# Sliding-window scores of the two later query blocks from stacked high and low parts, and the token rows reloaded later

## The chip, the cores and the metric

One core of one Trainium2 chip runs the whole program. The number is the device time of one execution in microseconds (us); the median of several executions is compared. The engines are TensorE (PE, its weight loads are listed apart as PEld), VectorE (DVE), ScalarE (ACT), GpSimd (POOL) and SyncE (SP, which here only issues DMAs).

## The reference, cut to what matters

512 tokens of width 1024 go through one decoder block. After an RMSNorm and an input projection come two groups of 8 query heads on 2 key heads each, head width 64. One is banded attention with a window of 128 and a sink per head; the other has a compressed, a selected and a window-512 branch. The part that is changed is the score product of the first group:

```
s = einsum('bnqhgd,bnkhd->bnhgqk', qb, kb) * (dh ** -0.5)     # 128 queries x 256 keys
s = where(mask, s, -inf)
p = softmax(concatenate([s, sink]))[..., :-1]
```

Then `x = x + mixed @ w_out`, and `x = x + peer_ffn(rmsnorm(x))`: products with 2 x 128 x 128 expert rows and a top-16 retrieval. All of it is float32.

## The kernel before

**Precision.** A product of two float32 tiles is either one plain float32 matmul, or some matmuls of type fp32r. For the latter an operand is split into a high part (ScalarE copies it to an fp32r tile) and a low part (the rest, by a subtraction). A head has only 64 rows, so the rows of a 128-row operand can hold a query's high part on one half and its low part on the other ("stacked"). Against the key's high part on both halves, and then the key's low part on both halves, two matmuls give the whole product.

**The attention loop.** 96 units run in one software pipeline, `UNITS`: query block qb = 0 to 3, then the branches SWA (the local attention), SEL, WIN, then 8 heads. Unit s = 24 qb + 8 branch + head. The score width is 128 or 256 for SWA (at most two key blocks), and 128 (qb + 1) for the others. So SWA units are s = 0 to 7, 24 to 31, 48 to 55 and 72 to 79. At step s:

- TensorE issues the scores of unit s into `bank[s % 3]` (`query_keys`: L1598 if packed, two matmuls; L1600 if plain, one matmul that the trace shows as two passes; then the mask, L1602), after `exp_done` of unit s-3. Then it transposes the probabilities of unit s-3 (L1671) and multiplies those of unit s-5 with the values (L1687). Between these lie the compressed branch's steps (L1632, L1697, L1703) and transposes of finished rows (L1646).
- VectorE takes the maximum of unit s (L1142 for SWA and then a minimum with the sink, L1143; L1146 for the others), and at even s copies the transposed probabilities of unit s-3 out of PSUM (L1211). Every eighth step it closes a group of 8 units (`finish`, L1114 to L1133). The compressed branch has L1177 and L1183.
- ScalarE takes the exponential of unit s (L761), and at odd s copies the transposed probabilities of unit s-3 (L780).

**Packing before.** Only SEL and WIN of query blocks 2 and 3 (widths 384 and 512) are packed: q in `qp`, k in `k_hi` and `k_lo`. The parts are made inside the loop, `PARTS` of them (4 of q, then 8 of k) at the steps `PACK_AT` = 12, 14, ..., 34. At each, ScalarE writes the high part on 64 partitions x 512 at the head of its step, before exp(s) (L741, L745), and GpSimd, in the order of `PARTS`, subtracts it to give the low part (L528, L533). For k, GpSimd waits until all four high parts of a key head are there (`pack_hi >= i + 4 - n`), so its subtractions come in runs of four. The first packed unit, s = 56, waits for all of `pack_lo`.

**Token rows.** `xt`, 16 KB of each partition, holds the token rows at the start. While attention runs it is first scratch of the compressed branch (`cx`, `hid_raw`, `hrep`). SyncE reloads x into it (`load_x`, L369, 2 MB) once `hrep` has been used (`cmp_ps >= 2`, step 6), then waits for the last score (`s_done >= 96`) and loads the next weight tile (L409). The first reader of the reloaded rows is the residual addition after the output projection, L1249.

Of the kernel before, what the change touches and what calls it, by code (L numbers as in the profile page):

```python
# [99 lines left out]
C_AT = [50 + 6 * qb for qb in range(TB)]  # L100
C_LATE = 2
PACKED = 2 * P
PARTS = [(w, g, n) for w in ("q", "k") for g in range(GROUPS) for n in (range(2) if w == "q" else range(4))]
PACK_AT = {12 + 2 * i: i for i in range(len(PARTS))}
M_AT = {74 + 5 * b + 2 * half: (b, half) for b in range(TB - 1) for half in range(2)}
W4_AT = {57 + 2 * k: k for k in range(KC)}

# [29 lines left out]
def build(nc, x, x_t, pos, params, consts, consts_b, consts_h, wts, wgate, w1, w2, subkeys, norms, down, rows, up, y):  # L137
# [80 lines left out]
    cx_parts = [place(f"cx_parts{i}", [P, LP, 2, GROUPS, NC], F32R, xt_at + i * 8192) for i in range(2)]  # L218
    w1_lo = [place("w1k_lo", [P, LP, CMP_HIDDEN], F32R, after_w), place("w1v_lo", [P, LP, CMP_HIDDEN], F32R, w1v_at)]
    w1_hi = [place("w1k_hi", [P, LP, CMP_HIDDEN], F32R, base + 32768), place("w1v_hi", [P, LP, CMP_HIDDEN], F32R, base)]  # L220
    glog_T = place("glog_T", [2 * N_GATES, T], F32, scratch)
    hid_raw = [place(f"hid_raw{i}", [2 * GROUPS * NC, 2 * CMP_HIDDEN], F32, xt_at + (1 + i) * 2048) for i in range(2)]
    hrep = place("hrep", [P, GROUPS * 2, 4, CP], F32, xt_at)
# [130 lines left out]
    with nc.Block() as block:  # L354

        @block.sync
        def _(sp):
# [32 lines left out]
            for i in range(1, TILES_IN + TILES_OUT + 2):  # L390
                if i == TILES_IN + TILES_OUT:
                    sp.wait_ge(S("mixed_done"), TB)
                    for e in range(DR):
                        load_down(e)
                    sp.dma_start(h_row[:], norms[1:2].partition_broadcast(P).rearrange("p o d -> p (o d)"))\
                      .then_inc(S("late_loaded"), 16)
                    sp.dma_start(sk[:], subkeys.rearrange("p (s k) -> p s k", s=2)).then_inc(S("late_loaded"), 16)
                if i >= 2:
                    used, count = tile_used(i - 2)
                    sp.wait_ge(S(used), count)  # L400
                if i == TILES_IN + 1:
                    sp.wait_ge(S("hrep_done"), 1)
                    sp.wait_ge(S("cmp_ps"), 2)
                    load_x()
                    sp.wait_ge(S("s_done"), len(UNITS))
                if i == TILES_IN:
                    sp.wait_ge(S("hid_done"), 2)
                w_i = wts[i].rearrange("p (k c) -> p k c", k=KC)
                sp.dma_start(w_raw[i % 2][:], w_i).then_inc(S(f"w_loaded{i % 2}"), 16)  # L409
                if i == 1:  # L410
                    sp.dma_start(wg_raw[:], wgate.rearrange("p (k c) -> p k c", k=KC)).then_inc(S("wg_loaded"), 16)
# [78 lines left out]
        def _(pool):  # L490
# [32 lines left out]
            for i, (what, g, n) in enumerate(PARTS):  # L523
                own = slice(DH * g, DH * g + DH)
                if what == "q":
                    other = slice(DH * (1 - g), DH * (1 - g) + DH)
                    pool.wait_ge(S("pack_hi"), i + 1)
                    nc.gpsimd.tensor_tensor(qp[g][other, 2 * n:2 * n + 2], qT[own, 1, 2 * n:2 * n + 2, PACKED:T],  # L528
                                            f32(qp[g][own, 2 * n:2 * n + 2]), ALU.subtract).then_inc(S("pack_lo"), 1)
                else:  # L530
                    to, br = slice(DH * (n // 2), DH * (n // 2) + DH), n % 2
                    pool.wait_ge(S("pack_hi"), i + 4 - n)
                    nc.gpsimd.tensor_tensor(k_lo[g][to, br], kT[own, 2 + br], f32(k_hi[g][own, br]), ALU.subtract)\  # L533
                        .then_inc(S("pack_lo"), 1)
# [54 lines left out]
        def _(act):  # L589
# [137 lines left out]
            for s in range(len(UNITS) + 13):  # L727
# [9 lines left out]
                if s in PACK_AT:  # L737
                    what, g, n = PARTS[PACK_AT[s]]
                    own = slice(DH * g, DH * g + DH)
                    if what == "q":  # L740
                        nc.scalar.activation(qp[g][own, 2 * n:2 * n + 2], qT[own, 1, 2 * n:2 * n + 2, PACKED:T], ACT.Copy)\  # L741
                          .then_inc(S("pack_hi"), 1)
                    else:
                        to, br = slice(DH * (n // 2), DH * (n // 2) + DH), n % 2
                        nc.scalar.activation(k_hi[g][to, br], kT[own, 2 + br], ACT.Copy).then_inc(S("pack_hi"), 1)  # L745
# [730 lines left out]
        def _(pe):  # L1476
# [102 lines left out]
            def query_keys(s):  # L1579
# [3 lines left out]
                n = width(qb, br)  # L1583
                k0 = (qb + 1) * P - n
                tok = slice(qb * P, (qb + 1) * P)
                if n > PACKED:
                    if s == min(u for u in range(len(UNITS)) if width(*UNITS[u][:2]) > PACKED):
                        pe.wait_ge(S("pack_lo"), len(PARTS))
                elif br == SWA:
                    q = (q_g1 if g else qT)[:, 0, j, tok]  # L1590
                else:
                    q = q_g1[:, 1, j, tok] if g else q_g0[:, j, tok]
                if s >= 3:
                    pe.wait_ge(S("exp_done"), s - 2)
                if n > PACKED:
                    q = qp[g][:, j, qb * P - PACKED:(qb + 1) * P - PACKED]
                    for x, kk in enumerate((k_hi[g], k_lo[g])):
                        nc.tensor.matmul(bank[s % 3][:, 0:n], q, kk[:, K_OF[br] - 2, k0:k0 + n], start=(x == 0), stop=False)  # L1598
                else:
                    nc.tensor.matmul(bank[s % 3][:, 0:n], q, kT[:, K_OF[br], k0:k0 + n], start=True, stop=False)  # L1600
                mw = n if br == SWA else P
# [338 lines left out]
```

## Time and profile before

| | |
|---|---|
| median of 3 runs | 1538.78 us (1537.42 to 1542.04) |
| the profiled execution, its own time | 1537.43 us |
| its span in the trace | 1535.6 us |
| TensorE / VectorE / ScalarE / GpSimd busy | 98% / 80% / 41% / 35% |
| attention loop in the trace | about 118 to 252 us |
| TensorE's granted clock | 1.00 in every stretch of the loop, the mean 0.997 |

The profiled execution lies 1.35 us below the median, and 1.8 us of it lie outside the span. Busy shares are averages over very unlike stages. "PE busy" in a window includes modelled ends of matmuls, so distances between the starts of matmuls are the safer measure of TensorE's pace.

### The profile page before, as it was taken

The numbers are of one execution on the slowest core, as the hardware profiler recorded it, in microseconds if no ns is written. First come the engines' busy times: TensorE is split into PE (matmuls) and PEld (weight loads), VectorE is DVE, ScalarE is ACT, GpSimd is POOL, SyncE is SP. The second block draws the span as 40 slices with busy tenths as digits, with TensorE's granted clock in tenths as the row PEclk, the third lists the DMA queues.
The fourth block names the chain that finished last, engine by engine and source line by source line (L and its number), as shares of the span: only waits on it lengthen the run. The fifth ranks groups of instructions, "written<-read, shape, count | busy, mean of one in ns | idle before, by whom it ended". The sixth has DMA issues, their size and how long they took to land.

```text
span 1535.6 us, 22620 instructions
## 1 busy us (share of the span) xinstructions
PE 1510.3 (98%) x8483; PEld 1347.4 (88%) x8483; DVE 1229.3 (80%) x2264; ACT 626.5 (41%) x1048; POOL 538.1 (35%) x359
## 2 busy tenths in 40 slices
PE   9999999999999999999999999999999999999997
PEld 6887888798889999998888888999999999999996
DVE  5567885439999999984776777888888889888885
ACT  6247565333222346663333333333333333333334
POOL 0322101055756720002111112555555555555521
PEclk9999999999999999999999999999999999999999
DMA  7302003224323548989999989999999999999961
GB/s 309 145 26 86 1 2 127 95 91 131 122 66 104 178 156 315 341 313 357 307 302 307 308 289 344 367 363 369 361 359 368 364 372 363 359 375 353 372 237 65
DMA packets 148508, 378.85 MB, mean 247 GB/s; under 512 B 11792, under 2 KB 76688, under 8 KB 145456
## 3 DMA queue, kind: packets, MB, share of 16 engines
q1 hardware_dynamic: 100544, 202.01, 37.8%
q0 software_dynamic: 37200, 138.56, 24.6%
q10 hardware_dynamic: 10656, 36.85, 6.5%
q8 instruction: 68, 1.11, 0.3%
q14 instruction: 40, 0.33, 0.1%
HBM read 338.50 MB, written 38.86 MB: 246 GB/s over the span
## 4 chain that ended last, share of the span: by engine, by line
PE 71%; DVE 24%; ACT 2%; DMA 2%; issue 1%; SPq 0%; DVEq 0%; ACTq 0%
PE bank L1847 22%; PE bank L1755 15%; PE bank L1853 11%; PE bank L1480 8%; PE bank L1762 7%; PE bank L1687 2%; DVE oh L1379 2%; DVE gp L1387 2%; DVE gp L1384 2%; DVE oh L1382 2%; DVE cand L1317 1%; PE bank L1671 1%; DVE d_lo L1368 1%; DVE key L1272 1%; DVE ti L1291 1%
## 5 line engine op out<-in xcount | busy, mean ns | idle before, releaser
L1755 PE MATMUL bank<-h_hi,d_hi 128*128 128x384 f32 x1024 | 349.8, 342 | 1.1 <-DVE h_lo L1233 1.1
L1755 PE MATMUL bank<-h_lo,d_hi 128*128 128x384 f32 x1024 | 345.3, 337 | 0.0
L577 POOL DMA_INDIRECT p_in<-rows,p_row x128 | 161.7, 1263 | 402.3 <-DVE p_dot L1406 183.3
L577 POOL DMA_INDIRECT p_in<-up,p_row x128 | 172.2, 1345 | 191.3 <-DVE p_dot L1406 97.0
L1762 PE MATMUL bank<-h_hi,d_lo 128*128 128x384 f32 x1024 | 200.1, 338 | 0.0
L1755 PEld LDWEIGHTS bank<-h_hi,d_hi 128*128 128x128 f32 x1024 | 192.9, 188 | 4.0 <-issue 1.3
L1755 PEld LDWEIGHTS bank<-h_lo,d_hi 128*128 128x128 f32 x1024 | 192.8, 188 | 3.2
L1847 PE MATMUL bank<-u_hi,w_hi_e 128*128 128x512 f32 x750 | 192.2, 391 | 0.3 <-DVE w_lo_e L1431 0.3
L1847 PE MATMUL bank<-u_hi,w_lo_e 128*128 128x512 f32 x750 | 191.0, 390 | 0.0
L1853 PE MATMUL bank<-u_lo,w_hi_e 128*128 128x512 f32 x750 | 190.9, 390 | 0.0
L1762 PEld LDWEIGHTS bank<-h_hi,d_lo 128*128 128x128 f32 x1024 | 180.9, 188 | 0.0
L1412 DVE SCALAR_TENSOR_TENSOR xt<-p_in,p_w,xt 128x1024 f32<-128x1024 f32 x128 | 164.0, 1281 | 5.6
L1847 PEld LDWEIGHTS bank<-u_hi,w_lo_e 128*128 128x128 f32 x750 | 140.8, 188 | 30.7
L1853 PEld LDWEIGHTS bank<-u_lo,w_hi_e 128*128 128x128 f32 x750 | 140.8, 188 | 29.2
L895 ACT ACTIVATE a_e<-bank 128x384 f32<-128x384 f32 x69 | 34.0, 492 | 323.6 <-PE bank L1762 323.6
L1363 DVE TENSOR_TENSOR u_lo<-u_raw,u_hi 128x1024 fp32r<-128x1024 f32 x128 | 156.4, 1223 | 11.0 <-ACT u_hi L869 10.6
L1426 DVE TENSOR_TENSOR a_e<-a_e,g_e 128x384 f32<-128x384 f32 x128 | 71.3, 557 | 115.6 <-ACT a_e L895 63.8
L1847 PEld LDWEIGHTS bank<-u_hi,w_hi_e 128*128 128x128 f32 x750 | 139.7, 188 | 25.8 <-ACT u_hi L869 0.7
L1406 DVE CUSTOM_DVE_ANT_0 p_in<-p_in,h_row 128x1024 f32<-128x1024 f32 x128 | 153.2, 1219 | 0.0
L538 POOL TENSOR_TENSOR d_lo<-d_raw,d_hi 128x1024 fp32r<-128x1024 f32 x35 | 89.2, 2556 | 171.4 <-ACT d_hi L793 171.4
L900 ACT ACTIVATE w_hi_e<-a_e 128x384 fp32r<-128x384 f32 x128 | 67.4, 526 | 194.9 <-DVE a_e L1426 191.6
L793 ACT ACTIVATE d_hi<-d_raw 128x1024 fp32r<-128x1024 f32 x128 | 134.4, 1052 | 29.9 <-ACT f_act L823 24.1
(289 smaller groups left out, 2462.5 us busy)
## 6 DMA issues: line engine op xcount, KB each, us to landing
d_raw<-down SPq DMA_DIRECT2D x128, 512.0 KB, 6.3
u_raw<-up SPq DMA_DIRECT2D x128, 512.0 KB
gates_dram<-ev ACTq DMA_DIRECT2D x12, 2048.0 KB, 7.5
g_e<-gates_dram SPq DMA_DIRECT2D x32, 768.0 KB
w_raw<-wts SPq DMA_DIRECT2D x9, 2048.0 KB, 8.6
act_dram<-f_act ACTq DMA_DIRECT2D x59, 192.0 KB
a_e<-act_dram SPq DMA_DIRECT2D x59, 192.0 KB
xt<-x_in SPq DMA_DIRECT2D x2, 2048.0 KB, 11.7
```

Source lines behind the costliest of these rows:

```text
L538: nc.gpsimd.tensor_tensor(d_lo[f % DR][:], d_raw[f % DR][:], f32(d_hi[f % DH_R][:]), ALU.subtract)\
L577: pool.indirect_dma_start(out=p_in[n % GR][:], out_offset=None, in_=rows if kind == "D" else up.rearrange("n p d -> (n p) d"), in_offset=b ...
L793: nc.scalar.activation(d_hi[e % DH_R][:], d_raw[e % DR][:], ACT.Copy).then_inc(S("d_hi_done"), 1)
L1363: V.tensor_tensor(u_lo[e % DR][:], u_raw[e % DR][:], f32(u_hi[e % UH][:]), ALU.subtract)\
L1406: V.tensor_tensor_reduce(out=rows_in[:], in0=rows_in[:], in1=h_row[:], scale=1.0, scalar=0.0, op0=ALU.mult, op1=ALU.add, accum_out=p_dot[: ...
L1412: V.scalar_tensor_tensor(xt[:, TDB], rows_in[:], p_w[:, p:p + 1], xt[:, TDB], ALU.mult, ALU.add)\
L1426: V.tensor_tensor(a_v, a_v, g_e[n % 3][:, :, e % GB], ALU.mult).then_inc(S("w_mul"), 1)
L1480: m = nc.tensor.matmul(out, a, b, start=(n == 0 and j == 0), stop=(n == last and j == 2))
L1755: nc.tensor.matmul(bank[6 + e % 2][:, 0:TD], d_hi[e % DH_R][:, k], h[:, k, 0:TD], start=(k == j == 0), stop=False)
L1762: m = nc.tensor.matmul(bank[6 + e % 2][:, 0:TD], d_lo[e % DR][:, k], h_hi[:, k, 0:TD], start=False, stop=(k == KC - 1))
L1847: nc.tensor.matmul(bank[2 * b + half][:], w[e % 3][:, b * P:(b + 1) * P], u_hi[e % UH][:, half * COLS:(half + 1) * COLS], start=(e == 0 an ...
L1853: m = nc.tensor.matmul(bank[2 * b + half][:], w_hi_e[e % 3][:, b * P:(b + 1) * P], u_lo[e % DR][:, half * COLS:(half + 1) * COLS], start=F ...
```

## The change

It packs the SWA scores of query blocks 2 and 3 too (units 48 to 55 and 72 to 79). Their parts, 4 of q (`qs`) and 4 of k (`ks_hi`, `ks_lo`), go ahead of the 12 old ones, so that `PACK_AT` now has the 20 steps 10, 12, ..., 48: new ones at 10 to 24, the old q parts at 26 to 32, the old k parts at 34 to 48. Unit 48 waits for 8 low parts, and unit 56 for all 20. The new tiles take the room of `xt`, so ScalarE waits for `cmp_ps >= 2` before the first, and SyncE reloads x only after the last SWA score (`s_done >= 80`).

```diff
--- before.py
+++ after.py
@@ -100,8 +100,9 @@
 C_AT = [50 + 6 * qb for qb in range(TB)]
 C_LATE = 2
 PACKED = 2 * P
-PARTS = [(w, g, n) for w in ("q", "k") for g in range(GROUPS) for n in (range(2) if w == "q" else range(4))]
-PACK_AT = {12 + 2 * i: i for i in range(len(PARTS))}
+PARTS = [(w, g, n) for w in ("qs", "ks") for g in range(GROUPS) for n in range(2)]
+PARTS += [(w, g, n) for w in ("q", "k") for g in range(GROUPS) for n in (range(2) if w == "q" else range(4))]
+PACK_AT = {10 + 2 * i: i for i in range(len(PARTS))}
 M_AT = {74 + 5 * b + 2 * half: (b, half) for b in range(TB - 1) for half in range(2)}
 W4_AT = {57 + 2 * k: k for k in range(KC)}
 
@@ -218,6 +219,9 @@
     cx_parts = [place(f"cx_parts{i}", [P, LP, 2, GROUPS, NC], F32R, xt_at + i * 8192) for i in range(2)]
     w1_lo = [place("w1k_lo", [P, LP, CMP_HIDDEN], F32R, after_w), place("w1v_lo", [P, LP, CMP_HIDDEN], F32R, w1v_at)]
     w1_hi = [place("w1k_hi", [P, LP, CMP_HIDDEN], F32R, base + 32768), place("w1v_hi", [P, LP, CMP_HIDDEN], F32R, base)]
+    qs = [place(f"qs{g}", [P, HPG, T - PACKED], F32R, xt_at + g * 4096) for g in range(GROUPS)]
+    ks_hi = [place(f"ks_hi{g}", [P, T], F32R, xt_at + 8192 + g * 2048) for g in range(GROUPS)]
+    ks_lo = [place(f"ks_lo{g}", [P, T], F32R, xt_at + 12288 + g * 2048) for g in range(GROUPS)]
     glog_T = place("glog_T", [2 * N_GATES, T], F32, scratch)
     hid_raw = [place(f"hid_raw{i}", [2 * GROUPS * NC, 2 * CMP_HIDDEN], F32, xt_at + (1 + i) * 2048) for i in range(2)]
     hrep = place("hrep", [P, GROUPS * 2, 4, CP], F32, xt_at)
@@ -401,6 +405,7 @@
                 if i == TILES_IN + 1:
                     sp.wait_ge(S("hrep_done"), 1)
                     sp.wait_ge(S("cmp_ps"), 2)
+                    sp.wait_ge(S("s_done"), STEP_QB * (TB - 1) + HEADS)
                     load_x()
                     sp.wait_ge(S("s_done"), len(UNITS))
                 if i == TILES_IN:
@@ -527,6 +532,17 @@
                     pool.wait_ge(S("pack_hi"), i + 1)
                     nc.gpsimd.tensor_tensor(qp[g][other, 2 * n:2 * n + 2], qT[own, 1, 2 * n:2 * n + 2, PACKED:T],
                                             f32(qp[g][own, 2 * n:2 * n + 2]), ALU.subtract).then_inc(S("pack_lo"), 1)
+                elif what == "qs":
+                    other = slice(DH * (1 - g), DH * (1 - g) + DH)
+                    pool.wait_ge(S("pack_hi"), i + 1)
+                    nc.gpsimd.tensor_tensor(qs[g][other, 2 * n:2 * n + 2],
+                                            (q_g1 if g else qT)[own, 0, 2 * n:2 * n + 2, PACKED:T],
+                                            f32(qs[g][own, 2 * n:2 * n + 2]), ALU.subtract).then_inc(S("pack_lo"), 1)
+                elif what == "ks":
+                    to = slice(DH * n, DH * n + DH)
+                    pool.wait_ge(S("pack_hi"), i + 2 - n)
+                    nc.gpsimd.tensor_tensor(ks_lo[g][to], kT[own, 0], f32(ks_hi[g][own]), ALU.subtract)\
+                        .then_inc(S("pack_lo"), 1)
                 else:
                     to, br = slice(DH * (n // 2), DH * (n // 2) + DH), n % 2
                     pool.wait_ge(S("pack_hi"), i + 4 - n)
@@ -737,7 +753,16 @@
                 if s in PACK_AT:
                     what, g, n = PARTS[PACK_AT[s]]
                     own = slice(DH * g, DH * g + DH)
-                    if what == "q":
+                    if PACK_AT[s] == 0:
+                        act.wait_ge(S("cmp_ps"), 2)
+                    if what == "qs":
+                        nc.scalar.activation(qs[g][own, 2 * n:2 * n + 2],
+                                             (q_g1 if g else qT)[own, 0, 2 * n:2 * n + 2, PACKED:T], ACT.Copy)\
+                          .then_inc(S("pack_hi"), 1)
+                    elif what == "ks":
+                        to = slice(DH * n, DH * n + DH)
+                        nc.scalar.activation(ks_hi[g][to], kT[own, 0], ACT.Copy).then_inc(S("pack_hi"), 1)
+                    elif what == "q":
                         nc.scalar.activation(qp[g][own, 2 * n:2 * n + 2], qT[own, 1, 2 * n:2 * n + 2, PACKED:T], ACT.Copy)\
                           .then_inc(S("pack_hi"), 1)
                     else:
@@ -1583,19 +1608,26 @@
                 n = width(qb, br)
                 k0 = (qb + 1) * P - n
                 tok = slice(qb * P, (qb + 1) * P)
-                if n > PACKED:
+                packed = n > PACKED or (br == SWA and qb * P >= PACKED)
+                if packed:
                     if s == min(u for u in range(len(UNITS)) if width(*UNITS[u][:2]) > PACKED):
                         pe.wait_ge(S("pack_lo"), len(PARTS))
+                    if s == STEP_QB * PACKED // P:
+                        pe.wait_ge(S("pack_lo"), 4 * GROUPS)
                 elif br == SWA:
                     q = (q_g1 if g else qT)[:, 0, j, tok]
                 else:
                     q = q_g1[:, 1, j, tok] if g else q_g0[:, j, tok]
                 if s >= 3:
                     pe.wait_ge(S("exp_done"), s - 2)
-                if n > PACKED:
-                    q = qp[g][:, j, qb * P - PACKED:(qb + 1) * P - PACKED]
-                    for x, kk in enumerate((k_hi[g], k_lo[g])):
-                        nc.tensor.matmul(bank[s % 3][:, 0:n], q, kk[:, K_OF[br] - 2, k0:k0 + n], start=(x == 0), stop=False)
+                if packed:
+                    late = slice(qb * P - PACKED, (qb + 1) * P - PACKED)
+                    if br == SWA:
+                        q, parts = qs[g][:, j, late], [kk[:, k0:k0 + n] for kk in (ks_hi[g], ks_lo[g])]
+                    else:
+                        q, parts = qp[g][:, j, late], [kk[:, K_OF[br] - 2, k0:k0 + n] for kk in (k_hi[g], k_lo[g])]
+                    for x, kk in enumerate(parts):
+                        nc.tensor.matmul(bank[s % 3][:, 0:n], q, kk, start=(x == 0), stop=False)
                 else:
                     nc.tensor.matmul(bank[s % 3][:, 0:n], q, kT[:, K_OF[br], k0:k0 + n], start=True, stop=False)
                 mw = n if br == SWA else P
```

## Rows read from the trace of the kernel before

**Rows 1.** The page: engines and lines of the chain that ended last.
```profile
PE 71%; DVE 24%; ACT 2%; DMA 2%; issue 1%; SPq 0%; DVEq 0%; ACTq 0%
```

**Rows 2.** Windows: stretch, length, busy us of PE, PEld, DVE, ACT, POOL; clock, DMA.
```profile
161.00:177.00 16.00, 16.00 (x122) 14.09 (x121) 13.25 (x41) 10.34 (x38) 0.00 (x0) 1.00 0.01 2
177.00:183.00 6.00, 4.61 (x37) 3.96 (x35) 5.32 (x14) 1.73 (x6) 0.00 (x0) 1.00 0.00 1
...
207.00:217.00 10.00, 10.00 (x83) 9.14 (x81) 6.89 (x19) 6.06 (x18) 0.00 (x0) 1.00 0.00 1
```

**Rows 3.** Timeline of PE, a plain SWA unit: start, us, line, operation.
```profile
207.71 0.65 PE L1600 MATMUL bank<-kT,qT 128*128 128x256 f32 x2
208.19 0.27 PE L1602 MATMUL bank<-cstb 128*128 128x256 bf16 x1
```

**Rows 4.** Timeline of PE, fp32r matmuls of 256 and of 384 columns.
```profile
107.10 0.38 PE L1513 MATMUL bank<-w1v_hi,cx_parts 128*124 128x256 f32 x1
107.32 0.28 PE L1513 MATMUL bank<-w1v_lo,cx_parts 128*124 128x256 f32 x1
107.44 0.28 PE L1513 MATMUL bank<-w1v_hi,cx_parts 128*124 128x256 f32 x1
...
188.79 0.42 PE L1598 MATMUL bank<-k_hi,qp 128*128 128x384 f32 x1
189.05 0.33 PE L1598 MATMUL bank<-k_lo,qp 128*128 128x384 f32 x1
189.22 0.23 PE L1602 MATMUL bank<-cstb 128*128 128x128 bf16 x1
```

**Rows 5.** The chain in order of time, around units 53 and 77: start, us, what.
```profile
177.26 0.12 PE bank L1602
...
182.26 0.41 PE bank L1671 x2
...
216.77 0.44 DVE nmax L1142
```

**Rows 6.** Timeline of DVE and POOL, and line L533's durations (ns, min/median/max).
```profile
143.55 0.67 DVE L1143 TENSOR_TENSOR nmax<-nmax,nsink 128x1 f32<-128x1 f32 x1
144.59 0.97 DVE L1143 TENSOR_TENSOR nmax<-nmax,nsink 128x1 f32<-128x1 f32 x1
...
157.40 1.23 DVE L1114 TENSOR_TENSOR coef<-rsum,es 128x8 f32<-128x8 f32 x1
...
141.72 5.05 POOL L533 TENSOR_TENSOR k_lo<-kT,k_hi 64x512 fp32r<-64x512 f32 x4 [5.51 <-ACT k_hi L745]
154.50 5.34 POOL L533 TENSOR_TENSOR k_lo<-kT,k_hi 64x512 fp32r<-64x512 f32 x4 [7.73 <-ACT k_hi L745]
...
L533 POOL TENSOR_TENSOR k_lo<-kT,k_hi x8: 1257/1266/1530, 141.7 to 158.6; 64x512 fp32r<-64x512 f32 x8
```

**Rows 7.** Timeline of PE, the masks of units 29, 30 and 40 to 42.
```profile
144.75 0.27 PE L1602 MATMUL bank<-cstb 128*128 128x256 bf16 x1
...
146.36 0.27 PE L1602 MATMUL bank<-cstb 128*128 128x256 bf16 x1
...
159.94 0.22 PE L1602 MATMUL bank<-cstb 128*128 128x128 bf16 x1
...
161.85 0.22 PE L1602 MATMUL bank<-cstb 128*128 128x128 bf16 x1
...
163.06 0.22 PE L1602 MATMUL bank<-cstb 128*128 128x128 bf16 x1
```

**Rows 8.** Line L745's durations, and a row of ACT's timeline (idle before it).
```profile
L745 ACT ACTIVATE k_hi<-kT x8: 620/628/632, 136.0 to 153.8; 64x512 fp32r<-64x512 f32 x8
...
131.86 0.37 ACT L761 ACTIVATE pr<-bank,nmax 128x128 f32<-128x128 f32 x1 [0.42 <-DVE nmax L1146]
```

**Rows 9.** DMA issue of x (KB each, us to landing), and its first reader.
```profile
xt<-x_in SPq DMA_DIRECT2D x2, 2048.0 KB, 11.7
...
L1249 DVE TENSOR_TENSOR xt<-xt,bank x8: 674/686/689, 266.0 to 302.3; 128x512 f32<-128x512 f32 x8
```

## The prediction

> **What bounds the kernel now.** I first read the chain of waits of the page: TensorE holds 71% of it and VectorE 24% [rows 1]. The attention loop is a small part of the span, but nothing after it can start without it, so a microsecond gained or lost there should be one at the end. The question is which engine sets the pace of each stretch of the loop. For that I read busy time by stretch, the chain piece by piece, and the starts of the mask matmuls, one for each unit.
>
> The reader is to see three things. Between 161 and 177 us TensorE is never idle, while VectorE is busy 13.25 of 16 us; between 177 and 183 us this turns round, 4.61 of 6 us for TensorE and 5.32 for VectorE [rows 2]. The chain changes engine there: from 177.4 us, the scores of unit 53 being ready, to 182.26 us it runs over VectorE (maximum, closing of a group, compressed branch), and TensorE then continues with the transposes of step 56. The same happens behind unit 77, at 216.77 us [rows 5]. So of the 16 units to be changed, 48 to 53 and 72 to 77 are on the chain with their TensorE time, 12 in all, and 54, 55, 78 and 79 are not.
>
> The third thing is small rows that are far too long. L1143, a minimum of one column, took 0.67 and 0.97 us, and L1114, eight columns, took 1.23 us [rows 6]. Normal is about 0.16 us for either (the 0.67 and 0.97 are above it by 0.51 and 0.81, the 1.23 by 1.07, in sum 2.4 us). All three lie inside a run of GpSimd subtractions, 141.72 to 146.77 and 154.50 to 159.84 us, and each ends where one of the subtractions ends (1.27 us each). They read both operands from SBUF; VectorE's instructions with one operand in PSUM, beside them, keep their length. I take it that such a VectorE instruction waits out the GpSimd instruction that is running. It also goes the other way: one L533 took 1530 ns where 1266 is the median [rows 6].
>
> The Trainium skill, page "SBUF — State Buffer", section "Who interferes with whom", says the same: a VectorE instruction with two SBUF inputs contends with a GpSimd instruction that reads SBUF, and the second to issue waits for the first to end. The trace agrees (0.67, 0.97 and 1.23 us, and 1530 ns). By that rule, which names no other case, the change would be charged as in the forecast below; were it not to hold, as in the first rival.
>
> **What a packed unit costs TensorE.** A plain unit takes 208.19 - 207.71 = 0.48 us from its first pass to its mask [rows 3]. For two fp32r matmuls of 256 columns there are two neighbours. In the compression, coming from plain matmuls, the first takes 0.22 us to the start of the second, and that 0.12 us: 0.34. The packed pair of 384 columns takes 0.26 + 0.17 = 0.43 us [rows 4]. The pair has 256 columns, so I take 0.34 us, and for the slightly earlier start behind L1687 nothing: a gain of 0.14 us a unit. The bound on the bad side is the 384-column price, a gain of 0.05 us; on the good side two matmuls at the later spacing, 0.24 us, a gain of 0.24. On the chain, 12 units: 12 x 0.14 = **1.7 us gained** (0.6 to 2.9). The mask is unchanged. In block 3 the cover for this is good: VectorE is busy only 6.89 of 10 us between 207 and 217 [rows 2], so six units' 0.8 us should be kept. In block 2 VectorE has 16 - 13.25 us free before it takes over, and the other six units' 0.8 us is kept only if nothing is added to VectorE.
>
> **ScalarE.** Eight packs of 0.63 us are added [rows 8]; since the list starts at 10 and ends at 48, the steps that had none before are 10 and 36 to 48. Queued behind a pack is exp(s), and the transposes and scores of step s+3 wait for that. The pack at 10 delays ScalarE by about 0.4 us in a stretch where it has little room, but the idle 0.42 us before exp at 131.86 us takes it up [rows 8]: 0.1 us, at most 0.6. At 36 to 48 ScalarE is busy 10.34 of 16 us [rows 2]; a pack every second step adds 0.63 per 2.3 us, 4.3 us over that stretch, which makes 14.7 of 16. It fits, barely, because exp(s) is wanted only three steps later. I put 0 on it, at most 1.
>
> **GpSimd's removed runs.** In the kernel before, subtractions run in the two groups of rows 6. What TensorE lost by them can be read off the masks: unit 30 came 1.61 us after unit 29 where 1.21 is the pace, and unit 41 came 1.91 us after 40 where 42 follows 41 by 1.21 [rows 7]. That is 0.40 + 0.70 = 1.1 us of the 2.4 us that VectorE lost, a share of 0.46. With the old k parts moved on, the second run no longer meets L1114 of step 37, and the first is replaced by single subtractions. If all is removed, **1.1 us gained**.
>
> **GpSimd's new places.** There are now 20 subtractions, 25.3 us at 1.27. They come singly after the packs at 10 to 16 and at 26 to 32, in pairs after 20 and 24, and in runs of four (about 5.1 us) after 40 and 48. VectorE's instructions with two SBUF operands at those steps, counted in the code: step 13 L1114; step 21 L1118; steps 24 to 31 eight L1143; steps 29 and 32, L1118, L1131, L1214 (15 or so in stretches where GpSimd works about half the time: 12 in number, 6 hit); steps 41 to 44 four L1183 and step 45 L1118; steps 48 to 52 five L1143 and L1192 (11, inside or at the edge of the runs: 10 hit). Sixteen hits at the mean wait of three before, 2.4/3 = 0.8 us, would be 12.8 us; the mean of a wait that begins anywhere in 1.27 us is 0.63, which gives 10 us. I take 0.63, as a wait is at most one subtraction. With the share 0.46 that reached TensorE before, **4.6 us lost**. The bounds: nothing, if VectorE's slack takes all up (its lag behind the masks was absorbed in more than half of the cases); 10 us if all reach TensorE. Most of it I expect at steps 41 to 52. There the pace was TensorE's, and a run that blocks L1183 and then L1143 turns it into VectorE's: one subtraction and one blocked 0.4 us instruction make 1.67 us for a step that took 1.2. ScalarE's packs lie in the same steps.
>
> **The waits on the parts.** Unit 48 needs the eighth low part, made about 20 steps earlier. Unit 56 needs the twentieth. Unit 48 lies some 6 to 7 us ahead of the mask of 53 at 177.26, so the last pack ends near 172 and four subtractions near 177; the scores of unit 56 come less than 2 us ahead of its step's transposes at 182.26 [rows 5]. The wait costs nothing, with about 3 us to spare; if the last run were stretched by more than that, TensorE would stand behind it with all transposes of the step queued.
>
> **The reload.** It is issued after unit 79, about 4 us behind the row at 216.77 [rows 5], lands 11.7 us later, near 233, and is first read at 266.0 us [rows 9]. SyncE has nothing queued between but the wait for the last score, after which its weight load is issued as before. 0 us, with some 30 us of cover.
>
> **The sum.** -1.7 (TensorE) + 0.1 (ScalarE) - 1.1 (old runs) + 4.6 (new runs) = +1.9 us. The profiled execution's 1537.43 would become 1539.3; on the median of 1538.78 it is 1540.7. I give **1540.5 us**. 0.3% of this kernel is 4.6 us; this is about what a measurement can tell from no change.
>
> **The rivals.**
> - *The gain lands* (chance 0.28). VectorE's slack and three units of distance absorb the waits on GpSimd, as they absorbed 54% of them before. For it: GpSimd's new singles are short and VectorE is idle up to 3 us of 10 in block 3. Against: VectorE had 2.75 us free in 16 where the runs now fall. The time: 1538.78 - 1.7 - 1.1 = 1536.0, with the good bound of a pair 1534.8.
> - *Slower by more than 0.3%* (0.07). One mechanism: the waits of VectorE on GpSimd reach TensorE nearly in full at steps 41 to 56, since ScalarE's packs have used up the slack there. 16 hits of 0.63 give 10 - 2.7 = +7.3 us, 1546.1. It decides from 11 or 12 hits on that pass through in full (4.6 + 2.7 = 7.3 us). Against it: less than half passed before.
> - *The pair is no cheaper* (0.07). At 0.43 us or more for a pair the change brings TensorE 0.6 us or less, and the lock stays: 1538.78 - 0.6 - 1.1 + 4.6 + 0.1 = 1541.8.
>
> **How the numbers follow.** The forecast has the remaining 0.58. The range reaches from near the first rival's time to between the forecast and the second: 1536.0 to 1544.0. All but the second rival lie within 4.6 us of now; a measurement's own scatter adds a little at either edge. Faster by over 0.3%: 0.03; within 0.3%: 0.90; slower by over 0.3%: 0.07.
>
> **What would show it.** In the profile after: L1598 with 256-column pairs about 0.34 us from first to mask; L1183 and L1143 rows above their 0.4 and 0.16 us wherever a GpSimd row lies beside them, some ten or more; L1114 of step 37 back at 0.16 us; TensorE's masks of units 41 to 52 further apart than 1.2 us; block 3's SWA units 0.14 us quicker each; the loop's end a little later than 252 us, or earlier if the first rival holds. The prediction is wrong if VectorE's long rows are few, if they are many and TensorE's masks keep their pace, or if anything behind the loop changes its length.

## The result and the profile after

| | before | after |
|---|---|---|
| median | 1538.74 us (1537.39 to 1542.04, 10 runs) | 1544.3 us (1541.51 to 1547.15, 10 runs) |
| the profiled execution, its own time | 1537.43 us | 1544.3 us |
| its span | 1535.6 us | 1542.5 us |
| attention loop, first mask to last | 129.2 us | 133.2 us |
| busy share TensorE / VectorE / ScalarE / GpSimd | 98 / 80 / 41 / 35% | 98 / 80 / 41 / 35% |

The ratio is 1.0034, 95% interval 1.0024 to 1.0043. The kernel became slower, clear of the scatter. Whether by more or by less than 0.3%, the size that the prediction set as its limit, the interval doesn't tell. The forecast of 1540.5 us lies 3.8 us below the median, and the range ended at 1544.0, 0.3 us below it.

The page's chain of the changed kernel, by engine, is nearly the same (before: [rows 1]):

```profile
PE 70%; DVE 24%; DMA 2%; issue 2%; ACT 1%; SPq 0%; ACTq 0%; DVEq 0%
```

The windows answer better to the question (columns as in [rows 2]):

```profile
124.00:131.00 7.00, 7.00 (x51) 6.60 (x52) 3.90 (x16) 4.13 (x20) 1.02 (x1) 0.76 0.01 2
...
161.00:177.00 16.00, 15.18 (x116) 12.78 (x115) 15.55 (x38) 12.51 (x38) 7.21 (x6) 1.00 0.01 2
177.00:183.00 6.00, 3.84 (x28) 3.35 (x28) 4.31 (x10) 2.49 (x10) 3.20 (x3) 1.00 0.01 1
...
207.00:217.00 10.00, 10.00 (x87) 9.29 (x86) 9.12 (x22) 6.61 (x21) 0.00 (x0) 1.00 0.01 2
...
306.00:314.00 8.00, 6.35 (x30) 5.92 (x29) 4.78 (x10) 2.32 (x5) 0.00 (x0) 0.79 0.73 265
```

Between 161 and 177 us VectorE went from 13.25 to 15.55 of 16 us busy, and TensorE, never idle before [rows 2], now is. Two stretches, at 124 and at 306 us, have a granted clock of 0.76 and 0.79.

The timeline of TensorE, around the steps 50 to 56 and in block 3:

```profile
175.22 0.36 PE L1630 MATMUL bank<-ks_hi,qs 128*128 128x256 f32 x1
...
175.42 0.28 PE L1630 MATMUL bank<-ks_lo,qs 128*128 128x256 f32 x1
...
175.54 0.28 PE L1634 MATMUL bank<-cstb 128*128 128x256 bf16 x1
...
177.50 0.41 PE L1703 MATMUL bank<-cst,pr 128*128 128x128 f32 x2 [0.47 <-ACT pt L805]
...
179.54 0.41 PE L1703 MATMUL bank<-cst,pr 128*128 128x128 f32 x2 [0.82 <-DVE pt L1236]
...
181.21 1.13 PE L1735 MATMUL bank<-vbd,c_pT 128*128 128x256 f32 x4 [0.87 <-ACT c_pT L796]
...
187.60 0.41 PE L1703 MATMUL bank<-cst,pr 128*128 128x128 f32 x2 [1.75 <-DVE pt L1236]
```

A packed unit takes 0.20 us to its second matmul and 0.12 to its mask, 0.32 in all, where a plain one takes 0.48 [rows 3]. In brackets stands TensorE's idle time: 0.47, 0.82 and 0.87 us at steps 51 to 53. From mask to mask, compared with before, the step of unit 53 is longer by 1.91 us, 25 by 0.63, 33 by 0.56, 49 by 0.50, 52 by 0.49 and 47 by 0.44; 41 is shorter by 0.76 us, 30 by 0.31, and 72 to 79 by 0.18 each, of which unit 81 gives back 0.36.

What VectorE does at these steps, and GpSimd beside it:

```profile
164.51 1.28 DVE L1208 TENSOR_TENSOR c_sc<-c_sc,cst 128x248 f32<-128x248 f32 x1
...
174.40 0.16 DVE L1168 TENSOR_TENSOR nmax<-nmax,nsink 128x1 f32<-128x1 f32 x1
...
175.70 0.78 DVE L1168 TENSOR_TENSOR nmax<-nmax,nsink 128x1 f32<-128x1 f32 x1
...
177.00 0.77 DVE L1217 TENSOR_TENSOR c_coef<-c_sum,gates 128x32 f32<-128x32 f32 x1
...
178.25 0.81 DVE L1168 TENSOR_TENSOR nmax<-nmax,nsink 128x1 f32<-128x1 f32 x1
...
164.25 5.48 POOL L549 TENSOR_TENSOR k_lo<-kT,k_hi 64x512 fp32r<-64x512 f32 x4 [7.73 <-ACT k_hi L770]
175.19 5.08 POOL L549 TENSOR_TENSOR k_lo<-kT,k_hi 64x512 fp32r<-64x512 f32 x4 [5.46 <-ACT k_hi L770]
```

L1168 is the minimum with the sink (L1143 before). At 174.40 us, before the run of subtractions, it takes 0.16 us; inside the run it takes 0.78 and 0.81. In all 14 VectorE rows of the loop are too long, by 9.40 us in sum, where before there were three and 2.4 us [rows 6]. The chain in order of time runs over these rows until TensorE's product L1735 of step 53. Of the L1168 row at 178.25 it has 0.07 us, and the rest of that row stands in it as "issue", time for which the profile shows no wait:

```profile
175.70 0.78 DVE nmax L1168
...
177.00 0.78 DVE c_coef L1217
177.80 0.43 DVE nmax L1167
178.25 0.07 DVE nmax L1168
...
180.89 0.28 ACT c_pT L796
181.21 1.13 PE bank L1735 x4
```

The reload stays covered, by these three rows of after (SyncE's timeline, the list of DMA issues, whose last column is the time to landing, and the first reader L1274): issued at 223.13 us, it is there 11.2 us later, 36 us before 270.4.

```profile
223.13 0.38 SPq L373 DMA_DIRECT2D xt<-x_in  x1
...
xt<-x_in SPq DMA_DIRECT2D x2, 2048.0 KB, 11.2
...
L1274 DVE TENSOR_TENSOR xt<-xt,bank x8: 675/686/689, 270.4 to 306.7; 128x512 f32<-128x512 f32 x8
```

### The profile page after: what moved, and what is told of

Read it like the earlier page. It is cut to its first block, busy times and chain, and to the rows that moved or that the text cites. A ratio compares the mean times of both kernels' runs of the same rounds, so it can differ in the third digit from the quotient of the medians.

```text
span 1542.5 us, 22638 instructions
## 1 busy us (share of the span) xinstructions
PE 1512.1 (98%) x8483; PEld 1349.2 (87%) x8483; DVE 1235.2 (80%) x2264; ACT 630.4 (41%) x1056; POOL 547.6 (35%) x367
## 3 DMA queue, kind: packets, MB, share of 16 engines
q8 instruction: 68, 1.11, 0.3%
## 4 chain that ended last, share of the span: by engine, by line
PE 70%; DVE 24%; DMA 2%; issue 2%; ACT 1%; SPq 0%; ACTq 0%; DVEq 0%
PE bank L1879 22%; PE bank L1787 15%; PE bank L1885 11%; PE bank L1505 8%; PE bank L1794 7%; PE bank L1719 2%; DVE oh L1404 2%; DVE gp L1412 2%; DVE oh L1407 2%; DVE gp L1409 2%; DVE cand L1342 1%; DVE d_lo L1393 1%; DMA w_raw<-wts 1%; PE bank L1703 1%; DVE key L1297 1%
## 6 DMA issues: line engine op xcount, KB each, us to landing
xt<-x_in SPq DMA_DIRECT2D x2, 2048.0 KB, 11.2
```

## The experiments

The table has all runs; "loop" is first mask to last in the one trace, in us, "at full clock" the same without the excess of the steps that lay in a stretch of lower granted clock (against the same steps of before, or for after_again of after), and "long rows" counts VectorE's over-long rows in the loop with their excess in us. The ratio is to the kernel before on the same chip, with its interval. Two cautions: the kernel before against itself came to 0.9992 (before_again), so a ratio within 0.001 of 1 says little; and the choice of the steps that count as slowed by the clock moves a value at full clock by up to 0.7 us (for after_again it would be 131.2 if unit 57, which came sooner behind the stretch, were left out).

| run | ratio | loop | at full clock | long rows |
|---|---|---|---|---|
| before | 1 | 129.2 | 129.2 | 3, 2.4 |
| after | 1.0034 [1.0024, 1.0043] | 133.2 | 131.8 | 14, 9.4 |
| after_again | 1.0030 [1.0017, 1.0043] | 132.8 | 131.9 | 14, 9.4 |
| before_again | 0.9992 [0.9982, 1.0002] | 130.5 | 129.2 | 3, 2.4 |
| reload_late | 0.9991 [0.9982, 1.0000] | 130.6 | 129.3 | 3, 2.4 |
| low_memset | 0.9993 [0.9984, 1.0002] | 128.5 | 127.1 | 0 |
| sink_scalar | 1.0025 [1.0016, 1.0034] | 135.2 | 130.2 | 6, 4.5 |
| plain_48 | 1.0024 [1.0016, 1.0033] | 134.9 | 132.0 | 14, 9.3 |
| singles | 1.0017 [1.0005, 1.0030] | 133.1 | 130.1 | 11, 5.7 |
| singles_scalar | 1.0021 [1.0012, 1.0030] | 129.6 | 129.6 | 6, 2.7 |
| block3_scalar | 1.0017 [1.0006, 1.0027] | 133.9 | 128.8 | 3, 2.2 |
| block3_moved | 1.0008 [0.9999, 1.0017] | 132.8 | 130.0 | 4, 2.4 |
| before_fix | 1.0009 [1.0000, 1.0018] | 128.9 | 128.9 | 2, 0.7 |
| delay_only | 1.0034 [1.0024, 1.0044] | 137.6 | not worked out | 3, 2.4 |

The theory: nearly all of the loss is VectorE's operations with two operands in SBUF waiting behind GpSimd's subtractions. The rivals: the reload, the packed pair itself, ScalarE's packs, and the granted clock.

**The reload alone (reload_late).** The kernel before with one line added:

```diff
                     sp.wait_ge(S("cmp_ps"), 2)
+                    sp.wait_ge(S("s_done"), STEP_QB * (TB - 1) + HEADS)
                     load_x()
```

> The kernel before with the later reload of x alone. The yardstick is the distance from the mask of unit 0 to that of unit 95 in the trace: 129.23 us before; 133.22 us with the change, of which 1.4 us lie in units 7 to 9 at a granted clock of 0.72 (131.8 us without these). Theory (waits of VectorE on GpSimd): the reload is hidden, loop 129.2 us, time within 1 us of before, ratio 0.9993 to 1.0007. Rival (the reload or its absence from 125 us costs something): the stretch at 124 to 130 us runs at the lower clock again, +1.4 us, or the residual additions behind the loop start late, ratio above 1.001.

The ratio is 0.9991, as good as the 0.9992 of the unchanged kernel. The stretch of lower clock near 124 us, the rival's sign, stood in this trace, but it stands in before_again too, without the line. The reload costs nothing that shows.

**The low parts without reading (low_memset).** The whole change, but GpSimd's subtractions of all four kinds become memsets; so the low parts of all packed scores are left out of the result. One of the four edits:

```diff
-                    nc.gpsimd.tensor_tensor(k_lo[g][to, br], kT[own, 2 + br], f32(k_hi[g][own, br]), ALU.subtract)\
+                    nc.gpsimd.memset(k_lo[g][to, br], 0.0)\
                         .then_inc(S("pack_lo"), 1)
```

> The change with all 20 low parts left out: GpSimd fills them with zeros (it writes, and reads nothing) in the same order and with the same waits. ScalarE's 20 packs and TensorE's pairs stay. Theory (VectorE's instructions with two SBUF operands wait for GpSimd's reads): no long VectorE rows, L1168 at 0.16 us and L1208 at 0.40 us throughout; the loop falls from 131.8 to 125.5 to 127 us (before's 1.2 us of stalls and up to 2.6 us of TensorE's gain come out), ratio to before 0.997 to 0.9985. Rival (ScalarE's eight more packs set the pace): the loop stays at 131 us or more, ratio 1.001 to 1.003.

The timeline of VectorE and GpSimd, this run:

```profile
173.78 0.20 DVE L1214 TENSOR_TENSOR c_coef<-c_sum,gates 128x32 f32<-128x32 f32 x1
...
174.47 0.16 DVE L1165 TENSOR_TENSOR nmax<-nmax,nsink 128x1 f32<-128x1 f32 x1
...
172.34 2.03 POOL L546 MEMSET k_lo<- 64x512 f32 x4 [7.50 <-ACT k_hi L767]
```

Beside a run of memsets (172.34 to 174.37) the same product with the gates takes 0.20 us instead of 0.77, and no row of the loop is long. The list of TensorE's waits in the loop, first of after, then of this run:

```profile
PE bank L1703 <- DVE pt L1236: 4.8, 8, 1.7
...
PE bank L1703 <- ACT pt L805: 2.1, 3, 1.2
...
PE bank L1735 <- ACT c_pT L796: 1.1, 2, 0.9
```

```profile
PE bank L1700 <- DVE pt L1233: 2.4, 3, 1.7
PE bank L1700 <- ACT pt L802: 1.6, 2, 1.2
...
PE bank L1732 <- ACT c_pT L793: 0.8, 2, 0.5
```

With the waits gone the loop at full clock is 4.7 us shorter than after's, 2.1 us shorter than before's, and the ratio is 0.9993 instead of 1.0034: 0.41% or 6.3 us. The loop came near its 125.5 to 127; the ratio missed its 0.997 to 0.9985. The memsets are shorter too (0.51 us each against 1.27), but TensorE waited for no low part in either kernel. The pair, the eight packs and the later parts are all still in it, so none of them is the loss. Two things differ beside the waits and no run separates them: the shorter GpSimd instructions, and zeros in the place of the low parts, which TensorE multiplies. For the loop, the runs below with true low parts point the same way.

**The sink's minimum with a scalar operand (sink_scalar).**

```diff
-                        V.tensor_tensor(nmax[:, s:s + 1], nmax[:, s:s + 1], nsink[:, h:h + 1], ALU.min)\
+                        V.tensor_scalar(nmax[:, s:s + 1], nmax[:, s:s + 1], nsink[:, h:h + 1], None, ALU.min)\
```

> The change, with the minimum of SWA's maximum and the sink (L1168) written so that the sink is a scalar operand, not a second tensor from SBUF. Theory: L1168 is at its normal length beside GpSimd's rows, L1208, L1217 and L1143 still wait; units 48 to 53 lose less, loop 131.8 to between 129.5 and 130.8 us. Rival (ScalarE's packs): 131.8 us as it is.

VectorE's timeline and GpSimd's:

```profile
178.09 0.83 DVE L1217 TENSOR_TENSOR c_coef<-c_sum,gates 128x32 f32<-128x32 f32 x1
...
179.41 0.21 DVE L1168 TENSOR_SCALAR nmax<-nmax,nsink 128x1 f32<-128x1 f32 x1
...
176.35 5.07 POOL L549 TENSOR_TENSOR k_lo<-kT,k_hi 64x512 fp32r<-64x512 f32 x4 [5.47 <-ACT k_hi L770]
```

Inside one and the same run of subtractions, the operation with two tensors waits (0.83 us) and the one with a tensor and a scalar does not (0.21 us; all 32 lie between 0.212 and 0.215). The loop at full clock is 1.6 us shorter than after's. The Trainium skill, page "SBUF — State Buffer", section "Who interferes with whom", draws the line at the same place, two SBUF inputs against a GpSimd instruction that reads SBUF and not against one that only writes it; both runs agree (0.21 us here, 0.16 us beside the memset). But the ratio is 1.0025, its interval overlaps that of after: see the clock, below.

**Query block 2 plain (plain_48).**

```diff
-                packed = n > PACKED or (br == SWA and qb * P >= PACKED)
+                packed = n > PACKED or (br == SWA and qb == TB - 1)
```

> The change with units 48 to 55 as plain products again, all parts still made; block 3 packed. Theory: between units 48 and 56 VectorE sets the pace, so TensorE's gain there was worth nothing, and the loop stays within 0.4 us of 131.8. Rival (TensorE's gain of 0.18 us a unit landed in block 2 as well): six to eight units, 1.1 to 1.4 us more, 132.9 to 133.2 us.

All parts are still made. The loop at full clock is 132.0 us against 131.8: packing block 2's eight units is worth 0.2 us, since VectorE sets the pace there, while block 3's eight steps are 1.46 us shorter in after (0.18 each), or 1.1 with what unit 81 gives back. Unit 81 does so in every run that packs block 3, plain_48 among them, and in none that doesn't.

**Subtractions one at a time (singles, singles_scalar).** The key parts are ordered so that each subtraction needs only its own high part; the second has the scalar minimum as well.

```diff
-                    pool.wait_ge(S("pack_hi"), i + 4 - n)
+                    pool.wait_ge(S("pack_hi"), i + 1)
```

> The change, with GpSimd's subtractions each right behind its own pack instead of in pairs and runs of four (the order of the packs within a key head is turned for that). The same 20 subtractions, 20 packs and pairs. Theory (what counts is which VectorE instructions with two SBUF operands GpSimd's subtractions fall on): L1208 and L1168 of units 49 to 52 are hit less than now, L1202 of steps 37 to 40 more; sum of the waits 5 to 8 us against 9.4, loop 131.8 to 129.5 to 131.3 us without stretches of lower clock. Rival (ScalarE's packs): 131.8 as it is.

> The same, and the sink as a scalar operand as in sink_scalar. Theory: only L1202, L1208, L1217 and the closings of groups can still wait; loop 128 to 130 us, near before's 129.2. Rival (ScalarE): 131 or more.

Runs of four broken up take the sum of the waits from 9.4 to 5.7 us and the loop at full clock from 131.8 to 130.1; with the scalar minimum 2.7 and 129.6. The ratios, 1.0017 and 1.0021, stay above 1.

**Only block 3 (block3_scalar, block3_moved).** Block 2's scores plain, six new parts instead of eight, behind the old ones, and the scalar minimum; the second moves them to steps at which VectorE was expected to have fewer operations with two tensors, and has the second key head's subtractions single.

```diff
-PACK_AT = {10 + 2 * i: i for i in range(len(PARTS))}
+PACK_AT = {12 + 2 * i if i < OLD else (46, 48, 50, 60, 62, 64)[i - OLD]: i for i in range(len(PARTS))}
```

(block3_scalar has `46 + 2 * (i - OLD)` there.)

> A candidate to beat both: only units 72 to 79 are packed. The 12 old parts stay at steps 12 to 34, and six new ones (2 of q for the last 128 tokens, 4 of k) go to steps 46 to 56; the sink is a scalar operand. Theory: TensorE's 8 x 0.18 us of block 3 stay (1.4 us less 0.4 given back at unit 81), the waits of L1143 in units 27 to 29 go, the one on the closing at step 37 stays, new subtractions may hit the c_coef product, the closing at step 53 and its additions (0 to 1.5 us): loop 127 to 129 us against 129.2, ratio 0.998 to 1.0. Rival (ScalarE's packs): loop 129.2 or more.

> Only block 3's scores are packed (query block 2 keeps its plain products); the six low parts that block 3 needs are made at other steps (46, 48, 50, 60, 62 and 64), the sink's minimum goes to VectorE as an operation with one tensor and a scalar, and key head 1's subtractions stay single. My theory (the price of the change is the wait of VectorE's two-tensor operations behind GpSimd's subtractions, and it counts where the maxima stand behind it): few or no long VectorE rows, the loop at the full granted clock 127 to 127.5 us against 129.2, and 0.9985 of the time before if no stretch of lower clock is added. The rival (TensorE's short idle stretches cost through the granted clock, wherever work moves): the loop at full clock is shorter but the ratio stays at 1.000 or above.

block3_scalar comes to 128.8 us at full clock, within its 127 to 129, but its ratio of 1.0017 missed the 0.998 to 1.0. block3_moved missed its 127 to 127.5: the last parts fell on the closing of a group at step 64. Its VectorE and GpSimd:

```profile
192.28 1.80 DVE L1229 TENSOR_TENSOR xs<-xs,o_tmp 128x512 f32<-128x512 f32 x1
...
194.47 1.28 DVE L1247 TENSOR_TENSOR w_lo<-w_raw,w_hi 128x512 fp32r<-128x512 f32 x1
...
192.26 2.94 POOL L545 TENSOR_TENSOR ks_lo<-kT,ks_hi 64x512 fp32r<-64x512 f32 x2 [17.12 <-ACT ks_hi L765]
```

Their excess is 1.11 and 0.60 us over the usual 0.69 and 0.68, and the steps of units 63 and 64 are longer by 1.10 and 0.60: here, with nothing between, all of it reached TensorE. Even so its ratio, 1.0008, is the lowest of all versions that pack anything with true low parts.

**The repair without the packing (before_fix).** The kernel before with the scalar minimum, and the second key head's subtractions single.

```diff
-                    pool.wait_ge(S("pack_hi"), i + 4 - n)
+                    pool.wait_ge(S("pack_hi"), i + 1 if g else i + 4 - n)
```

> The kernel before, with no packing of the two later blocks; only the sink's minimum written with one tensor and a scalar, and key head 1's subtractions single. My theory: the loop at full clock 127.9 to 128.2 us against 129.2, and a ratio near 0.999. The rival: as in the run with the whole change, the time is taken back by stretches of lower clock, and the ratio is 1.000 to 1.002.

Units 30 and 41 came 0.40 and 0.76 us sooner, 33 and 34 took 0.36 back, and the loop was 0.3 us shorter, not 1.0. Two VectorE rows are long there, at 146.80 and 147.96 us; in low_memset, which has no such rows, 33 and 34 take nothing back. The ratio is 1.0009, so the forecast of 0.999 missed. So no version found beats the kernel before.

**A small stall alone (delay_only).** The kernel before, with 18 additions on VectorE at step 58, on a tile that nothing reads any more.

> The kernel before, with 18 chained additions on a dead tile put into VectorE's step 58, some 4 us in which TensorE runs dry and nothing else is changed. The question is why the change costs 5.3 us by the medians where its loop is only 2.6 us longer at equal clock. Theory (a later second half meets a lower clock once more often, near 310 us): loop +3.3 to 4.3 us, the granted clock falls between 306 and 316 us in this trace as with the change, mean clock over its runs 0.0005 to 0.001 below before's, time up by 1 to 1.5 us more than the loop. Rival (the extra belongs to the change itself): time up by as much as the loop, clock as before.

Its windows:

```profile
190.00:195.00 5.00, 2.82 (x23) 2.37 (x22) 4.48 (x18) 0.65 (x3) 0.00 (x0) 1.00 0.00 0
195.00:202.00 7.00, 6.30 (x30) 5.37 (x30) 5.99 (x13) 4.37 (x12) 0.00 (x0) 0.53 0.01 2
```

TensorE was idle 2.2 of 5 us and then ran at a granted clock of 0.53, near the lower of its two levels. 30 matmul rows lie in those 7 us, where 153 to 170 lie in 22 us at full clock. The ratio is 1.0034: no subtraction was added here and no row became long, and yet it costs what the whole change costs, 5.2 us. TensorE's waits for the copied probabilities there are 3.6 us, against 1.4 in the kernel before. The theory missed in three of its terms: the loop of this trace is 8.4 us longer, not 3.3 to 4.3 (4.9 us at units 61 to 65 and 3.5 at units 3 to 10, around a stretch of half clock such as other traces have near 124 us); the clock near 310 us stayed at 1.00; and the mean clock is 0.0019 lower, not 0.0005 to 0.001. The rival, the clock as before, missed too.

**Both kernels once more (after_again, before_again).**

> The changed kernel once more, for the scatter of a profile. If the stretches of lower granted clock belong to the kernel, its trace has them again near 125 and 310 us, and the ratio is again 1.003 to 1.004. If they fall by chance, they stand elsewhere or are missing, with the loop at 131 to 133 us.

> The kernel before once more. If the stretches of lower clock belong to the change, none near 125 and 310 us here, the loop 129.2 us and the ratio 1.000. If they fall by chance, one stands near 125 us here too, as in two other kernels with the block's work unchanged, and the ratio is still within 0.001 of 1.

The same windows, first before_again, then after_again:

```profile
124.00:131.00 7.00, 7.00 (x52) 6.68 (x52) 3.86 (x16) 3.88 (x19) 0.00 (x0) 0.76 0.68 250
```

```profile
124.00:131.00 7.00, 6.87 (x63) 6.26 (x63) 5.10 (x20) 5.35 (x26) 2.26 (x2) 1.00 0.00 0
...
177.00:183.00 6.00, 4.31 (x22) 3.59 (x20) 3.43 (x10) 2.23 (x9) 1.87 (x2) 0.77 0.02 4
...
306.00:314.00 8.00, 6.66 (x43) 6.41 (x44) 4.29 (x11) 3.01 (x7) 0.00 (x0) 1.00 0.74 271
```

The stretch near 124 us is in the kernel before too, and absent from after_again; the one at 310 us is absent as well, and another stands near 180. Where such a stretch falls changes from one execution to the next. The loop at full clock repeats within 0.1 us for both kernels (129.2 and 129.2, 131.8 and 131.9). So of each pair of cases the one that has them fall by chance holds for these two traces.

## Why the prediction was right or wrong, point by point

The direction and most of the mechanism were right, the size was not: +1.7 us was forecast and +5.2 measured by the ratio, which is the upper edge of the range. That the range reached so far is luck: it was drawn towards a rival in which the waits pass in full, and they did not.

- **What bounds the loop, and where: right.** VectorE takes over earlier, in block 2, as its windows show.
- **The packed unit: the size of a pair right, what it is worth less.** 0.34 was forecast, 0.32 to 0.33 measured; with the earlier start the step is 0.18 us shorter, not 0.14. But the term "12 x 0.14 = 1.7 us" counted six units of block 2 that gave 0.2 us; block 3's eight steps gave 1.46, and 1.1 with the 0.36 that unit 81 gives back. So 1.3 us of the 1.7 came.
- **ScalarE: right within what shows.** low_memset has all eight packs and its loop is 2.1 us shorter than before's; the forecast's terms without the new waits come to 1.7 - 0.1 + 1.1 = 2.7. Most of the missing 0.6 is that of the point above: in low_memset block 3 and unit 81 together gave 1.1 us, and units 48 to 57 together nothing.
- **The old runs removed: right.** Forecast 1.1 us; in low_memset, where nothing comes in their place, units 30 and 41 gave 0.40 and 0.76, 1.16 us, and no later step took it back. In after they gave 0.31 and 0.76, and unit 33 was 0.56 us later, beside the long rows of the new single subtractions.
- **The new waits: right.** Sixteen hits and 10 us forecast, 14 and 9.4 us measured; in low_memset 4.7 us of loop hang on them (4.6 forecast), a share of 0.5 (0.46 forecast). In the loop the rival "the gain lands" is refuted, and so is the one that has the waits pass in full, though the time it was to give, +7.3 us, lies nearer to the measured 5.2 than the forecast does. That the pair is no cheaper is refuted by its 0.32 us.
- **The waits on the parts and the reload: right**, nothing. GpSimd's last subtraction ends at 180.27 us (175.19 + 5.08), and the scores of unit 56 start at 185.18.
- **The loop as a whole.** +1.9 forecast, +2.6 measured at full clock (twice). The new waits (4.7 for 4.6) and the old runs came as forecast; most of the 0.7 is the gain of the pair.
- **The step that failed: from the loop to the time.** The prediction took a microsecond in the loop as one at the end, and granted clock 1.00 as given [rows 2]. By the ratio the time rose by 5.2 us (4.6 in after_again), and the loop gives 2.6 of them. The mean granted clock goes with the time: in the executions on record, 246 with a clock, one of the same kernel with a mean clock lower by 0.001 is about 1.0 us longer. But what lowers it is not settled. It is 0.9948 over after's runs, 0.9947 over after_again's and 0.9938 in delay_only and sink_scalar, against 0.9953 to 0.9962 for before in the different calls and 0.9955 in low_memset. That fits a price of short waits. plain_48 with all of the long rows has 0.9952, though, and before_fix, with fewer long rows than before, 0.9945. Against before's 0.9953 to 0.9956 after and after_again lie 0.0006 to 0.0008 lower, an estimated 0.6 to 1.2 us (the upper end takes 0.0008 of 1540 us as lost, the lower 1.0 us for each 0.001). That leaves at least 5.2 - 2.6 - 1.2 = 1.4 us without a place in the loop.

In the traces a part of the difference lies behind the loop, in code that the change doesn't touch. From the last mask to the end of the span it is 1287.7 and 1286.3 us in the two traces of before, and 1290.3 and 1288.6 in those of after. The first of after has one stretch of half clock more there; after_again has one fewer than before_again and is longer all the same. The list of TensorE's waits between 600 and 1000 us, of before_again and then of after_again (us, times, longest):

```profile
PE bank L1820 <- DVE gp L1387: 0.5, 1, 0.5
```

```profile
PE bank L1852 <- DVE gp L1412: 1.8, 2, 0.9
PE bank L1879 <- DVE w_lo_e L1456: 1.7, 2, 1.1
```

TensorE's idle time between 600 and 1000 us is 0.5 to 3.5 us in the fourteen traces, 1.5 and 0.5 in those of before and 2.3 and 3.5 in those of after. Whether the change shifts it or it falls by chance, two traces of each cannot tell.

What is shown: the loss hangs on GpSimd's subtractions, and in the loop on the waits behind them, since with the subtractions turned into memsets (low_memset) the long rows are gone and the ratio falls from 1.0034 to 0.9993; and a stall with no such wait can cost as much (delay_only). What is only argued: the split of the 5.2 us between loop and clock, which rests on a few traces and on means of a clock given to three digits. Open: the last 1.4 us, and what lowers the mean clock. That low_memset, whose loop is 2.1 us shorter, gives back only 0.0007 of the time (1.1 us), and before_fix nothing, is a gap of about 1 us, the size by which the kernel before differs from itself.

## What to carry to other kernels

When work is moved to GpSimd beside a VectorE that is nearly full, count the VectorE instructions with two SBUF operands that it will meet, at half a GpSimd instruction each (here 14 hits made 9.4 us, 0.67 each, at 1.27 us a subtraction), and look for a form with one tensor and a scalar. A gain in a stretch is worth something only if the engine that gets faster sets the pace there (1.1 us for eight units in block 3, 0.2 in block 2). And where TensorE is busy 98% of the time, a new idle piece of a microsecond or two may cost more than its length (in delay_only 2.2 us more of waiting cost 5.2 us): before a number goes in, run a small pure delay at that place to learn the rate.

## What the hardware showed unexpectedly

- **Short stretches at half clock inside a busy kernel.** In after, TensorE sat idle 0.58 and 1.07 us and then fell to half clock; its timeline:

```profile
306.81 1.09 PE L1751 MATMUL bank<-cst,xs 128*128 128x128 f32 x8 [0.58 <-DVE xs L1281]
308.97 0.42 PE L1787 MATMUL bank<-h_hi,d_hi 128*128 128x384 f32 x1 [1.07 <-DVE h_lo L1258]
...
309.42 0.53 PE L1787 MATMUL bank<-h_hi,d_hi 128*128 128x384 f32 x1
309.74 0.53 PE L1787 MATMUL bank<-h_lo,d_hi 128*128 128x384 f32 x1
```

From 309.42 on the matmuls of 384 columns start 0.32 us apart, 1.2 GHz instead of 2.4. In after_again the same two waits are there:

```profile
306.28 1.09 PE L1751 MATMUL bank<-cst,xs 128*128 128x128 f32 x8 [0.56 <-DVE xs L1281]
308.44 0.42 PE L1787 MATMUL bank<-h_hi,d_hi 128*128 128x384 f32 x1 [1.07 <-DVE h_lo L1258]
```

and the granted clock stays at 1.00 from 306 to 314. The kernel before has the pieces as well, 0.58 us before 302.39 and 1.07 before 304.55, at a clock of 1.00. The same idle pieces can be followed by a stretch at half clock or not. It was in the traces of three of the four runs with the full set of subtractions in their old order (after, plain_48, sink_scalar), and in none of the ten others, which is suggestive and no more. Between 549 and 557 us such a stretch stands in eleven of the fourteen traces, those of before among them.
- **The wait also stretches a large operation.** An addition of 512 columns that takes 0.69 us took 1.80 us in block3_moved beside two subtractions, which themselves took 2.94 us instead of 2.5.
